# A three-branch mixer trunk on one core: x loaded by features, the latents turned off TensorE, and another order of the start

## The reference

```python
h = rms_norm(x, norm_g[l]);  p = h @ w_in[l]          # 2048 x 12,480 columns
# A: stick-breaking attention, 4 heads x 128, strictly causal
# B: latent attention: q = rms_norm(c_q) @ w_uq, kv = rms_norm(c_kv) @ w_ukv (latents of 512),
#    per-head RMS norm, rotary part of 64, block-causal softmax, 8 heads
# C: RWKV-7: token shift, decay and rate through low-rank latents, 8 heads x 64, a state updated
#    token by token, group norm, bonus
g_sb, g_mla, g_rw = sigmoid(p_gate)                   # three gates of 2048
merged = g_sb*(y_sb @ w_br_sb) + g_mla*(y_mla @ w_br_mla) + g_rw*(y_rw @ w_br_rw)
x = x + merged @ w_out[l]
```

## Time and profile before

| | us |
|---|---|
| median of 3 runs | 1691.61 (1690.33 to 1692.4) |
| the profiled execution's own time | 1692.25 |
| its span, first to last instruction | 1690.5 |
| busy: PE / PEld / DVE / ACT / POOL | 1677.6 / 1399.2 / 1134.9 / 836.6 / 487.8 |
| DMA | 332.82 MB, mean 197 GB/s |

### The profile page before, as it was taken

How to read it: one execution, slowest core, us unless ns; L and a number is a source line. 1 busy time by engine, 2 the same in 40 slices (tenths; PEclk the granted TensorE clock), 3 DMA queues, 4 the chain that set the end, 5 groups by cost and what they waited for, 6 DMA issues and landing times.

```text
span 1690.5 us, 22088 instructions
## 1 busy us (share of the span) xinstructions
PE 1677.6 (99%) x8394; PEld 1399.2 (83%) x8394; DVE 1134.9 (67%) x1579; ACT 836.6 (49%) x1181; POOL 487.8 (29%) x722
## 2 busy tenths in 40 slices
PE   8999999999999999999999999999999999999999
PEld 7878888888888888888888788888888888888887
DVE  5668575766976566886656775756669666578853
ACT  6454453435544455554454454434445554555532
POOL 1011212410343426362410112233203534244500
PEclk9999999999999999999999999999999999999999
DMA  8865655655666557785687555556556565668754
GB/s 277 243 193 182 175 177 170 184 165 173 178 184 176 173 164 234 236 302 188 205 269 226 176 186 172 187 152 188 174 167 178 167 178 177 192 212 279 267 193 157
DMA packets 176913, 332.82 MB, mean 197 GB/s; under 512 B 19516, under 2 KB 32746, under 8 KB 176808
## 3 DMA queue, kind: packets, MB, share of 16 engines
q1 hardware_dynamic: 167048, 297.86, 57.7%
q0 software_dynamic: 9584, 33.48, 5.7%
q10 hardware_dynamic: 176, 0.07, 0.0%
HBM read 311.20 MB, written 16.78 MB: 194 GB/s over the span
## 4 chain that ended last, share of the span: by engine, by line
PE 92%; DVE 3%; ACT 2%; DMA 2%; issue 1%; SPq 1%; ACTq 0%; DVEq 0%
PE D L707 83%; PE B L707 8%; DMA ring<-in_w_in 2%; DVE w_lo L1398 1%; ACT w_hi L1026 1%; DVE xy L1398 0%; ACT arena L1026 0%; ACT gev L1026 0%; PE B L898 0%; DVE arena L1398 0%; DVE gev L1444 0%; PE B L877 0%; SPq L435 0%; ACT L1026 0%; DVE arena L1428 0%
## 5 line engine op out<-in xcount | busy, mean ns | idle before, releaser
L1398 DVE TENSOR_TENSOR w_lo<-ring,w_hi 128x1024 fp32r<-128x1024 f32 (+3 forms) x560 | 675.7, 1219 | 342.1 <-ACT w_hi L1026 334.0
L1026 ACT ACTIVATE w_hi<-ring 128x1024 fp32r<-128x1024 f32 (+3 forms) x560 | 575.0, 1038 | 463.9 <-PE D L707 361.5
L707 PE MATMUL D<-w_hi,ht_hi 128*128 128x512 f32 (+2 forms) x1728 | 681.3, 394 | 3.0 <-DVE w_lo L1398 2.8
L707 PE MATMUL D<-w_hi,ht_lo 128*128 128x512 f32 (+2 forms) x1728 | 666.0, 385 | 0.0
L707 PE MATMUL D<-w_lo,ht_hi 128*128 128x512 f32 (+2 forms) x1728 | 665.1, 385 | 0.0
L707 PEld LDWEIGHTS D<-w_hi,ht_hi 128*128 128x128 f32 x1728 | 325.1, 188 | 71.4 <-issue 7.8
L707 PEld LDWEIGHTS D<-w_hi,ht_lo 128*128 128x128 f32 x1728 | 324.5, 188 | 65.3
L707 PEld LDWEIGHTS D<-w_lo,ht_hi 128*128 128x128 f32 x1728 | 325.2, 188 | 59.0 <-issue 0.5
L609 POOL COPY arena<-arena 32x256 f32<-32x256 f32 x240 | 163.1, 680 | 144.7 <-DVE arena L1428 109.3
L707 PEld LDWEIGHTS B<-arena 128*66 128x66 f32 (+3 forms) x1312 | 134.2, 165 | 24.3 <-issue 8.2
L707 PE MATMUL B<-arena 128*66 128x64 f32 (+7 forms) x1312 | 144.7, 263 | 0.6 <-ACT arena L1026 0.6
(11 more groups left out here) (160 smaller groups left out, 1376.9 us busy)
## 6 DMA issues: line engine op xcount, KB each, us to landing
ring<-in_w_in SPq DMA_DIRECT2D x368, 512.0 KB, 4.5
ring<-in_w_out SPq DMA_DIRECT2D x64, 512.0 KB, 5.2
ring<-in_w_br_mla SPq DMA_DIRECT2D x32, 512.0 KB, 5.2
gate_spill<-gev POOLq DMA_DIRECT2D x24, 512.0 KB, 4.7
arena<-gate_spill POOLq DMA_DIRECT2D x24, 512.0 KB, 5.2
ring<-in_mla_w_ukv SPq DMA_DIRECT2D x16, 512.0 KB, 4.0
ring<-in_w_br_rw SPq DMA_DIRECT2D x16, 512.0 KB, 5.2
ring<-in_w_br_sb SPq DMA_DIRECT2D x16, 512.0 KB, 5.2
```

Source lines behind the costliest of these rows:

```text
L707: return nc.tensor.matmul(o, a, b, start=start, stop=stop, skip_group_check=True)
L1026: return nc.scalar.activation(o, i, fn, **kw)
L1398: return v.tensor_tensor(o, a, b, op)
```

## The change

- x comes a second time, transposed on the host in layout only (`xt`, four pieces of 128 partitions by 4 KB), and the norm's weights as columns (`gain_cols`). ScalarE's queue asks for the weights' columns, the four pieces and the identity; SyncE's asks for the first weight chunks at once.
- At the start TensorE transposes nothing. ScalarE and VectorE split XT two columns at a time before each narrow chunk. x itself is loaded by SyncE ahead of chunks 9 to 12, and its squares are taken behind the splits of chunks 12 to 15. AT_LORA moves from 16 to 17.
- The constants are asked for after the shift of rk, the rows and low-rank matrices at chunk 20 and not 12.
- The latents are turned by VectorE (two 32 x 32 block transposes) and moved by GpSimd (16 copies each) in pairs 1 and 2; ScalarE's and VectorE's splits of them come before pair 3.
- In a pair the product of AM and v of both halves comes at the end of level 5, the first half into B[0], the second into B[3]; one step of a pair fewer, and the steps' lengths are set anew.
- Some semaphores of each layer become one that counts on.

```diff
-AT_LORA = END["wk"] + 8
+AT_LORA = END["wk"] + 9
-RW_STEPS = [1, 1.2, 1, 1.5, 1.8] + [0.88, 0.98] * LEVELS + [0.85] * 6
-LATENT_STEPS = [2, 2.5]
+RW_STEPS = [1, 1.2, 1, 1.5, 1.8] + [0.9, 1] * LEVELS + [0.98] * 5
+LATENT_STEPS = [1.2, 1.1, 1.3, 1.2]
-RW_PE, RW_ACT, RW_DVE, RW_POOL = 8 + 2 * LEVELS, 5 + LEVELS, 5 + 2 * LEVELS, 9
+RW_PE, RW_ACT, RW_DVE, RW_POOL = 7 + 2 * LEVELS, 5 + LEVELS, 5 + 2 * LEVELS, 9
+        XT = [arena[:, j * 1024:(j + 1) * 1024] for j in range(3)] + [arena[:, at_mkv:at_mkv + 1024]]
+        LAT_TURNED = [S1, PV[:, :, 512:1024]]
...
 # SyncE
-            for j in range(4):
-                first_x(j)
-                if j < LEAD:
-                    first_chunk(j)
+            for j in range(LEAD):
+                first_chunk(j)
+                    if l == 0 and 2 * RING < n <= 3 * RING:
+                        first_x(n - 2 * RING - 1)
-                    if n == 3 * RING:
+                    if n == 5 * RING:
                         row(GR[:, 0:QK], mla_qn_g[l], rows_in[l])
...
 # GpSimd
-                if l == 0:
-                    pool.wait_ge(split_lo, END["wk"] + 2)
-                    pool.dma_start(con[:, P:K_END], consts[:, P:K_END]).then_inc(con_in, 16)
+                    if l == 0 and i == 1:
+                        pool.dma_start(con[:, P:K_END], consts[:, P:K_END]).then_inc(con_in, 16)
+                def move_latents(i, d):
+                    turned = LAT_TURNED[i].rearrange("p h (k j t) -> p h k j t", k=4, j=4)
+                    moved = LAT_MOVED[i].rearrange("p k (h i t) -> p h k i t", h=2, i=4)
+                    if d == 0:
+                        pool.wait_ge(lat_turned, 2 * l + i + 1)
+                    for i0 in range(4):
+                        j = (i0 + d) % 4
+                        nc.gpsimd.tensor_copy(moved[32 * j:32 * j + 32, :, :, i0, :],
+                                              turned[32 * i0:32 * i0 + 32, :, :, j, :]).then_inc(lat_quarters, 1)
...
                     for n in range(1, LEVELS_IN - 1):
                         pool.wait_ge(rw_pe, 4 * RW_PE * l + RW_PE * p + 1 + 2 * n)
                         rw_level(p, n + 1)
                         beat(2)
+                        if p in (1, 2):
+                            pool.wait_ge(rw_pool, 4 * RW_POOL * l + RW_POOL * p + 7 + n)
+                            move_latents(p - 1, n)
...
 # TensorE
+                    if n == LEVELS:
+                        for h in range(HALVES):
+                            v = R[:, h, 1024 + p * P:1024 + (p + 1) * P]
+                            for a in range(2):
+                                mm((B[0], B[3])[h][:, h * P + 64 * a:h * P + 64 * a + 64], AM[:, 2 * a + h, 256:384],
+                                   v[:, 64 * a:64 * a + 64], a == 0, True)
-                    for j in range(4):
-                        pe.wait_ge(x_moved[j], 16)
-                        ...
-                        transposes((2 * j, 2 * j + 1), j * 512, first_pe)
+                    dense_to(END["wk"])
+                    pe.wait_ge(id_in, 16)
...
 # ScalarE
+            act.dma_start(ng, gain_cols[0]).then_inc(first_gain, 16)
+            for j in range(4):
+                act.dma_start(XT[j], xt[j].rearrange("p (k t) -> p k t", k=4)).then_inc(xt_in[j], 16)
             act.dma_start(con[:, 0:P], consts[:, 0:P]).then_inc(id_in, 16)
+            def first_columns_hi(c):
+                act.wait_ge(xt_in[c // 2], 16)
+                for k in (2 * c, 2 * c + 1):
+                    last = f(hth[:, k, :], XT[k // 4][:, k % 4, :], scale=ng[:, k:k + 1])
+                last.then_inc(first_xh, 1)
+                    for c in range(KD // KC):
+                        first_columns_hi(c)
+                        if c < LEAD:
+                            first_split(c)
+                        else:
+                            dense_to(c + 1 - LEAD)
+                    dense_to(END["wk"] - 1)
+                    while at[0] < END["wk"] + 5:
+                        at[0] += 1
+                        split(at[0] + LEAD - 1)
+                        if at[0] > END["wk"] + 1:
+                            first_squares(2 * (at[0] - END["wk"]) - 4, 2 * (at[0] - END["wk"]) - 3)
...
 # VectorE
+                for i, t in enumerate((CQ, CKV)):
+                    v.transpose(LAT_TURNED[i], t).then_inc(lat_turned, 1)
+                    dense_to(END["wk"] + 5)
                     sum_squares(first_sq, first_sum, 8)
```

More of the change, by code:

```diff
@@ L362, in program @@
         gn_var, gn_rs, gn_done = one("gn_var"), one("gn_rstd"), one("gn_done")
-        lat_act, lat_dve, lat_pe, lat_hi, lat_out = (sem("latents_" + n) for n in (
-            "rstd", "normed", "transposed", "hi", "lo"))
+        lat_act, lat_hi, lat_out = (sem("latents_" + n) for n in ("rstd", "hi", "lo"))
+        lat_turned, lat_quarters, lat_moved = (one("latents_" + n) for n in ("turned", "quarters_moved", "moved"))
         ml_sq, ml_ss, ml_rs, ml_turned = (one("ml_" + n) for n in ("squares", "sums", "rstd", "turned"))
@@ L386, in program @@
         first_gain, first_hi, first_lo = (one("first_" + n) for n in ("gains", "weights_hi", "weights_lo"))
-        gain_rows, gain_columns = one("gain_rows_in"), one("gain_columns")
+        xt_in = [one(f"columns_of_x_in{j}") for j in range(4)]
         first_pe, first_xh, first_xl, first_sq, first_sum = (s[-1] for s in (xt_pe, xt_act, xt_dve, x_sq, x_sum))
@@ L845, in rw_pair @@
                     if h:
[L846 to L850, removed]
+                        mm(B[3][:, P:2 * P], TT[:, 1, 0:P], ST, False, True).then_inc(rw_pe, 1)
+                        beat()
                     pe.wait_ge(rw_act, 4 * RW_ACT * l + a0 + LEVELS + 2 + 2 * h)
@@ L867, in rw_pair @@
                     beat()
[L869 to L879, removed]
             def mla_pair(p):
@@ L987, in _ @@
                 for p in range(4):
-                    if p == 1:
-                        latents()
+                    if p in (1, 3):
+                        beat(2)
                     rw_pair(p)
@@ L1149, in rw_pair @@
                     beat()
+                    if n == LEVELS:
+                        act.wait_ge(rw_pe, 4 * RW_PE * l + e + 2 * LEVELS + 2)
+                        f(YU[:, 0:P], B[0][:, 0:P]).then_inc(rw_act, 1)
                     beat()
                 for h in range(HALVES):
-                    for k in range(2):
-                        act.wait_ge(rw_pe, 4 * RW_PE * l + e + 2 * LEVELS + 3 + 3 * h + k)
-                        f(YU[:, k * P:(k + 1) * P], B[k][:, 0:P]).then_inc(rw_act, 1)
+                    for k in range(1 - h, 2):
+                        act.wait_ge(rw_pe, 4 * RW_PE * l + e + 2 * LEVELS + 2 + 3 * h + k)
+                        f(YU[:, k * P:(k + 1) * P], B[1][:, 0:P] if k else B[3][:, P:2 * P]).then_inc(rw_act, 1)
                         beat()
@@ L1331, in _ @@
                         latents()
+                    if p == 3:
+                        latents_hi()
                     rw_pair(p)
@@ L1732, in renewed_lo, with first_columns_lo @@
                     last.then_inc(xt_dve[l], 1)
+            def first_columns_lo(c):
+                dve.wait_ge(first_xh, c + 1)
+                for k in (2 * c, 2 * c + 1):
+                    last = v.scalar_tensor_tensor(htl[:, k, :], XT[k // 4][:, k % 4, :], ng[:, k:k + 1],
+                                                  hth[:, k, :].bitcast(F32), ALU.mult, ALU.subtract)
+                last.then_inc(first_xl, 1)
             def sum_squares(squared, done, count=4):
@@ L1917 @@
         args.append(nc.dram_tensor("in_" + name, a.shape, mybir.dt.from_np(a.dtype), kind="ExternalInput").ap())
+    x, gains = np.asarray(inputs["x"]), np.asarray(inputs["norm_g"])
+    columns = {"in_xt": x[0].T.reshape(4, 4, P, SEQ).transpose(0, 2, 1, 3).reshape(4, P, 4 * SEQ),
+               "in_gain_cols": gains.reshape(DEPTH, KD, P).transpose(0, 2, 1)}
     arrays["in_consts"] = constants()
     args.append(nc.dram_tensor("in_consts", (P, K_END), F32, kind="ExternalInput").ap())
+    for name, a in columns.items():
+        arrays[name] = np.ascontiguousarray(a)
+        args.append(nc.dram_tensor(name, a.shape, F32, kind="ExternalInput").ap())
     args.append(nc.dram_tensor("out_x", (1, SEQ, DM), F32, kind="ExternalOutput").ap())
```

131 lines of the change are left out of this document (53 added, 78 removed).

## The result

The kernel after takes 1699.5 us (median of five runs, 1697.79 to 1699.71), the kernel before 1691.61 (of five too, 1690.33 to 1692.4) on the same chip: ratio 1.0046, 95% interval 1.0034 to 1.0058. It is slower by 7.9 us. I had said 1693.0, in a range of 1688 to 1698. The profiled executions differ by 7.3 us (spans 1697.8 and 1690.5), so the traces hold nearly all of it.

A forecast was written before the change was run, and what follows sets the result against it. The prediction took TensorE's instruction stream plus the start to bound the kernel. Latents -3.5, pairs -0.2 and start +5.1 summed to +1.4 us, from 1691.61 to 1693.0 us, with an 8-in-10 range of 1688 to 1698.

The forecast's parts named there:

- the mark: At the start: the start of weight chunk 17 on TensorE, 50.72 us before; a delay still there stays to the end.
- Loads (L = 33.8): Start: an earlier request but 2 MB more to load; chunk 12 lands at 33.8 us, near the 34.12 of before.
- L: Landing time of weight chunk 12 at the start; 34.12 us before, forecast 31.0 at best and 39.0 at worst.
- the request of chunk 8 at 15.0: Start: chunk 8's load may be asked for once chunk 4 is split; taken at 15.0 us.
- (a): Start: x and weights share the DMA engines, so L is 37 to 39; slower, 1697 us, chance 0.31 with (c).
- The chain behind L (L + 22.0): Start, after L: squares, memsets, shift DMA, VectorE, four transposes; chunk 17 starts at L + 22.0, +5.1 us.
- Latents (-3.5): Both layers: sixteen transposes a layer leave TensorE, 1.75 us each layer, -3.5 us in all; GpSimd's copies fit its idle time.
- pairs (-0.2): Eight pairs: one group of small matmuls fewer in each; between 0 and 0.7 us saved, -0.2 taken.
- (b): Start: the shift is not last, so the mark comes at L + 17.4; faster, 1687.0 us, chance 0.15.
- (c): Pairs: GpSimd's copies hold up tables and matmuls, four slips of 2.8 us; 1704 us, chance 0.02 within (a)'s side.
- The sum: Whole kernel: -3.5 - 0.2 + 5.1 = +1.4 us, giving 1693.0 us for the median.

## Why the prediction was wrong

- **What bounds the kernel, and the mark.** Right: outside the start the time is TensorE's stream, and what is lost at the mark stays lost.
- **Loads (L = 33.8).** Mis-sized by 2.1 us: 35.92. Its first step failed, the request of chunk 8 at 15.0; it came at 16.83, since chunk 1 landed at 11.01 and chunk 4 was split only at 16.76. That is the mechanism of rival (a), the two queues sharing the DMA engines, but not its size: L lies between mine and (a)'s 37 to 39, just over the 35.8 from which I had let (a) decide. The rule of the Trainium skill behind (a) (DMA: Bandwidth & Descriptors, Queues, rings and completion order) fits the 8.53 of the one queue against 11.01; weighed by it, my L would have been too late. The rate I took was right, 332 GB/s against 331 in 20 to 45 us: 16.83 + 2.0 + 16.8 is 35.6.
- **The chain behind L (L + 22.0).** Right: L + 21.6, in the order foreseen, squares, memsets, shift, VectorE, four transposes (0.71 us of it at half clock, where I had 0.35).
- **The clock: a term that was missing.** This is the step that failed most. I priced the wait itself and took TensorE behind it at full pace, without a reason. In the profiled execution the granted clock was at 0.50 for 6.8 us and chunk 17 took 2.5 us longer, the largest part of the miss there. I had used the slow pace at the start, hidden there, and did not ask what the new idle time would do to it. In the medians this price is not shown: with the wait filled they give 1698.81, still outside my range.
- **Latents (-3.5) and pairs (-0.2).** Mis-sized by 1.7 us in the trace: 2.0 came back behind chunk 18. About 1.4 us of that went to VectorE, which GpSimd's copies slow, by the traces with and without the copies; I had asked only whether the copies fit into GpSimd's idle time. They do. A gap of 0.7 us from one matmul to the next in the later part is there with and without the copies (at 649.33 in the kernel after, at 638.81 with the copies cut); it comes with the new places in the plan and was not followed further.
- **Rivals.** (b) is out: the shift was last. (c) in its form, tables late, is out; the slips came by way of VectorE and were small. (a) gave 1697 and had 0.31 of my chance; its number is nearer to 1699.5 than mine, partly by luck, for its L was too late and it had no clock term either. Only the lora products moved away from the wait, the time comes out almost as my sum has it (1693.3 for 1693.0), but by errors that cancel, which is luck: 3.5 us late at chunk 20 instead of 5.1, and a smaller return.
- **The sum.** Over 1693.0, by the traces: L and its chain +1.7, clock +2.5, latents and pairs +1.7, and 0.6 that the medians differ by beyond the profiled executions: 6.5 us.

## What to carry to other kernels

When an edit puts a wait of a few microseconds in front of TensorE, ask what the fallen clock may take behind it (up to 2.5 us in a trace here), and look first whether the work that waits can be put some chunks later: one number gave back 6.2 of 7.9 us. When work moves off TensorE onto GpSimd, look at VectorE's short operations of that stretch and whether they are in the chain; idle time on GpSimd doesn't tell. A profile is one execution: see where it stands among the others before a difference of 2 us is read from it. A load put on a second queue beside the first chunks takes its share of the engines at once: it is worth asking which of the two is needed first.

## What the runs showed of the hardware

- The granted clock fell to 0.50 behind waits of TensorE for line 967 of 2.0, 3.1, 3.3 and 5.3 us (the kernel with x early, the kernel after, x's columns on one queue, mu late), for 3.4, 6.8, 6.8 and 3.4 us. A longer wait did not bring a longer slow stretch. Behind a wait of 1.54 us ahead of chunk 11 (the kernel with the lora products later) the clock did not fall.
- Under GpSimd's copies of 32x256 VectorE's six operations of 128x31 took 1.75 us instead of 1.18; under copies of 32x32, 1.22.
- At the very start the granted clock in the rows doesn't tell the pace: in the kernel after it reads 1.00 from 8.2 to 10.8 us, where matmuls of 128x256 start 0.21 us apart, against 0.12 from 12.7 us on.
- A second slow stretch of the kernel after, 35.36 to 38.77 us, lies behind the wait for chunk 11. It cost nothing at the mark of this trace, because TensorE had to wait for the shift anyway.
